# Latent attention with a paged cache: paged values and scores are moved directly behind the prompt's values, on TensorE

## The reference

```python
def latent_attention(q_abs, q_pe, c_kv, k_pe, q_pos, k_pos, w_uv):
    s = (jnp.einsum('bqhc,bkc->bhqk', q_abs, c_kv) + jnp.einsum('bqhr,bkr->bhqk', q_pe, k_pe)) * ATTN_SCALE
    s = jnp.where((k_pos[None, :] <= q_pos[:, None])[None, None], s, NEG_INF)
    p = jax.nn.softmax(s, axis=-1)
    o_lat = jnp.einsum('bhqk,bkc->bqhc', p, c_kv)
    return jnp.einsum('bqhc,chv->bqhv', o_lat, w_uv)
```

## Time and profile before

| | us |
|---|---|
| three runs, median (lowest, highest) | 2506.13 (2505.72, 2509.56) |
| span of the profiled execution, first to last instruction | 2500.6 |
| median less that span (the profiled execution has no time of its own beside its span) | 5.5 |
| attention loop, layer 1 (218.4 to 462.3) | 243.9, TensorE busy 235.9 |
| attention loop, layer 2 (1460.0 to 1704.3) | 244.3, TensorE busy 235.9 |

### The profile page before, as it was taken

One profiled execution on the slowest core, in us unless ns is written; L12 is line 12 of the kernel. 1 busy time (PEld: TensorE's weight loads), 2 busy tenths in 40 slices (PEclk: granted clock), 3 DMA queues, 4 the chain that ended last, 5 costly groups with the idle time before them and its releaser, 6 DMA issues.

```text
span 2500.6 us, 47127 instructions
## 1 busy us (share of the span) xinstructions
PE 2445.4 (98%) x18500; PEld 2197.3 (88%) x18500; DVE 1527.6 (61%) x1986; ACT 1025.4 (41%) x1535; POOL 926.5 (37%) x395
## 2 busy tenths in 40 slices
PE   8999999999999999999999999999999999999998
PEld 6996666897999999999979966668989999999998
DVE  5546666348776557655674566663497675567646
ACT  3224555327533333433441246552274333333334
POOL 2331000122664666455213310002136654665451
PEclk9999999999999999999999999999999999999999
DMA  6114322314545544663431143222236356445644
GB/s 224 55 39 119 94 86 81 119 59 149 199 161 213 204 157 152 214 217 142 148 113 50 35 130 89 87 87 109 75 126 252 145 182 232 165 151 180 223 141 154
DMA packets 182347, 347.40 MB, mean 139 GB/s; under 512 B 33969, under 2 KB 46449, under 8 KB 181425
## 3 DMA queue, kind: packets, MB, share of 16 engines
q1 hardware_dynamic: 116128, 207.12, 24.9%
q10 hardware_dynamic: 63504, 129.77, 14.3%
q0 software_dynamic: 2560, 8.39, 1.2%
HBM read 292.94 MB, written 49.06 MB: 137 GB/s over the span
## 4 chain that ended last, share of the span: by engine, by line
PE 81%; DVE 7%; ACT 4%; POOLq 3%; issue 2%; DVEq 1%; DMA 1%; POOL 1%; SPq 0%; ACTq 0%
PE psum L2926 21%; PE psum L2973 20%; PE psum L2428 12%; PE psum L2618 4%; PE psum L2413 3%; PE psum L2644 3%; PE psum L2458 3%; PE psum L2630 2%; PE psum L2521 2%; PE psum L2665 2%; PE psum L2477 2%; PE psum L2381 1%; ACT z L1174 1%; PE psum L2488 1%; PE psum L2678 1%
## 5 line engine op out<-in xcount | busy, mean ns | idle before, releaser
L2973 PE MATMUL psum<-hidh,wh 128*128 128x264 f32 x1312 | 374.2, 285 | 8.4 <-issue 5.9
L2973 PE MATMUL psum<-hidl,wh 128*128 128x264 f32 x1312 | 373.6, 285 | 0.0
L2973 PE MATMUL psum<-hidh,wl 128*128 128x264 f32 x1312 | 372.7, 284 | 0.0
L2926 PE MATMUL psum<-hh,wh 128*128 128x264 f32 x1280 | 363.4, 284 | 0.1
L2926 PE MATMUL psum<-hh,wl 128*128 128x264 f32 x1280 | 362.8, 283 | 0.0
L2926 PE MATMUL psum<-hl,wh 128*128 128x264 f32 x1280 | 362.6, 283 | 0.0
L2134 DVE TENSOR_TENSOR z<-psum,z 128x528 f32<-128x528 f32 x336 | 226.9, 700 | 94.1 <-PE psum L2973 94.1
L2973 PEld LDWEIGHTS psum<-hidh,wh 128*128 128x128 f32 x1312 | 246.5, 188 | 10.4 <-issue 7.0
L2973 PEld LDWEIGHTS psum<-hidh,wl 128*128 128x128 f32 x1312 | 247.2, 188 | 0.0
L2973 PEld LDWEIGHTS psum<-hidl,wh 128*128 128x128 f32 x1312 | 246.9, 188 | 0.0
L2926 PEld LDWEIGHTS psum<-hh,wh 128*128 128x128 f32 x1280 | 240.5, 188 | 0.5 <-issue 0.5
(11 more groups left out here) (329 smaller groups left out, 5935.0 us busy)
## 6 DMA issues: line engine op xcount, KB each, us to landing
hh<-h_quarters ACTq DMA_DIRECT2D x60, 1056.0 KB, 5.4
hl<-h_quarters ACTq DMA_DIRECT2D x60, 1056.0 KB, 7.5
raw<-wst SPq DMA_DIRECT2D x48, 512.0 KB, 3.6
z<-cache_c SPq DMA_DIRECT2D x352, 64.0 KB, 1.8
x<-x_spill SPq DMA_DIRECT2D x4, 4224.0 KB, 14.5
sacc<-wst SPq DMA_DIRECT2D x56, 256.0 KB, 3.2
t<-wst SPq DMA_DIRECT2D x56, 256.0 KB, 3.0
cn<-wst SPq DMA_DIRECT2D x56, 256.0 KB, 3.9
```

The lines of the kernel that those rows point to most:

```text
L2926: ins = pe.matmul(psum[:, up_bank(st, u) + q, 0:HW], w[:, o:o + P], m[part], start=(fresh and k == 0 and n == 0), stop=(k == 3 and n == 2) ...
L2973: ins = pe.matmul(psum[:, 2 * u + q, 0:HW], w[:, o:o + P], m[:, t, k * HB + q * HW:k * HB + q * HW + HW], start=(fresh and k == 0 and n == ...
```

## The change

On TensorE `step_values(c - 1)` moves from the end of phase 0 to directly behind `values`, and `step_scores(c)` from the end of phase 2 to directly behind `values` (at c = 0 and 8 behind `new_values`, which also moves forward). So tiles of 64 columns are followed by tiles of 32. `short` is dropped: `step_turn(c)` always stands in phase 3, and there `scores(i + 2, 1)` moves behind it. Bank 6 is divided by columns: prompt values in 0 to 127, paged values in 128 to 255. The paged matmuls no longer wait for bank 6 to be read; `values` still waits for both readers, and ScalarE's `take_o` now also waits for the paged values behind the prompt's, so that it does not read the bank while TensorE writes it. On VectorE phase 2 does `normalise`, `step_max`, then `take_pt` and `maxima`, instead of `take_pt`, `normalise`, `maxima`, `step_max`. On ScalarE `step_exp` moves from phase 3 to the end of phase 2.

```diff
@@ -279,6 +279,7 @@
 
         psum = ctx.enter_context(nc.psum_tensor("psum", [P, 8, 512], F32))
         ps = [psum[:, i, :] for i in range(8)]
+        prompt_o, paged_o = ps[6][:, 0:P], ps[6][:, P:2 * P]
 
         S = {}
 
@@ -1178,7 +1179,12 @@
 
                     u, j = JOBS[k]
                     act.wait_ge(o_full.sem, at.value(o_full, k + 1))
-                    act.activation(hh[:, u, tok(j)], ps[6][:, 0:P], ACT.Copy).then_inc(o_hi.sem, 1)
+                    c = (k + 1) // 2
+                    if k % 2 and k < len(JOBS) - 1:
+                        act.wait_ge(do_full.sem, at.value(do_full, out_of_step(c - 1)))
+                    if k % 2 == 0 and c % CHUNKS == 0:
+                        act.wait_ge(do_full.sem, at.value(do_full, out_of_step(c) - 1))
+                    act.activation(hh[:, u, tok(j)], prompt_o, ACT.Copy).then_inc(o_hi.sem, 1)
 
                 def take_pt(i):
 
@@ -1260,8 +1266,9 @@
                             if c == 0:
                                 act.wait_ge(outs.sem, at.value(outs, 64))
                             new_pt(c // CHUNKS)
+                    if ph == 2:
+                        step_exp(c)
                     if ph == 3:
-                        step_exp(c)
                         if i in K_AT and K_AT[i][1] == 0:
                             more_keys(K_AT[i][0])
                         step_pt(c)
@@ -1911,7 +1918,7 @@
 
                     u, j = JOBS[k]
                     dve.wait_ge(o_hi.sem, at.value(o_hi, k + 1))
-                    dve.tensor_tensor(hl[:, u, tok(j)], ps[6][:, 0:P], hh[:, u, tok(j)].bitcast(F32),
+                    dve.tensor_tensor(hl[:, u, tok(j)], prompt_o, hh[:, u, tok(j)].bitcast(F32),
                                       ALU.subtract).then_inc(o_new.sem, 1)
 
                 def take_pt(i):
@@ -1954,7 +1961,7 @@
                     dve.wait_ge(dexp.sem, at.value(dexp, first))
                     dve.tensor_copy(stat[:, 23:24], stat[:, 14:15])
                     dve.wait_ge(do_full.sem, at.value(do_full, first))
-                    dve.tensor_copy(oacc[quad], ps[6][:, 0:P]).then_inc(do_free.sem, 1)
+                    dve.tensor_copy(oacc[quad], paged_o).then_inc(do_free.sem, 1)
                     dve.drain()
 
                 def step_max(c):
@@ -1981,7 +1988,7 @@
                     quad = c // CHUNKS
                     dve.wait_ge(do_full.sem, at.value(do_full, out_of_step(c)))
                     dve.scalar_tensor_tensor(out=oacc[quad], in0=oacc[quad], scalar=stat[:, 6 + s:7 + s],
-                                             in1=ps[6][:, 0:P], op0=ALU.mult, op1=ALU.add).then_inc(do_free.sem, 1)
+                                             in1=paged_o, op0=ALU.mult, op1=ALU.add).then_inc(do_free.sem, 1)
                     dve.drain()
                     if c % CHUNKS == CHUNKS - 1:
                         dve.reciprocal(stat[:, 22:23], stat[:, 23:24])
@@ -2009,9 +2016,12 @@
                     big = JOBS[k][1] >= 4
                     if i % 2 == 0 and k > 0:
                         take_o(k - 1)
+                    if ph == 2:
+                        normalise(i + 1)
+                        step_max(c)
                     if big:
                         take_pt(i)
-                    if i + 1 < HALVES:
+                    if ph != 2 and i + 1 < HALVES:
                         normalise(i + 1)
                     if ph == 0 and c > 0:
                         take_ropes(c)
@@ -2027,10 +2037,8 @@
                             step_out(c - 1)
                         if c % CHUNKS == 0:
                             new_max(c // CHUNKS)
-                    if ph == 2:
-                        step_max(c)
-                        if c % CHUNKS == 0:
-                            new_out(c // CHUNKS)
+                    if ph == 2 and c % CHUNKS == 0:
+                        new_out(c // CHUNKS)
                     if ph == 3:
                         if i in K_AT and K_AT[i][1] == 1:
                             more_keys(K_AT[i][0])
@@ -2641,7 +2649,7 @@
                     pe.wait_ge(do_free.sem, at.value(do_free))
                     for kb in range(j + 1):
                         for e in range(2):
-                            ins = pe.matmul(ps[6][64 * e:64 * e + 64, 0:P],
+                            ins = pe.matmul(prompt_o[64 * e:64 * e + 64, :],
                                             vals[:, kb, (2 * u + e) * VD:(2 * u + e) * VD + VD],
                                             pts[2 * e + kb // 4][:, kb % 4, :], start=(kb == 0), stop=(kb == j),
                                             skip_group_check=True, tile_position=(0, 64 * e))
@@ -2678,10 +2686,6 @@
                     pe.matmul(ps[7][:, :], qrd[:, quad, :], rtt, start=False, stop=True,
                               skip_group_check=True).then_inc(ds_full.sem, 1)
 
-                def short(c):
-
-                    return c < STEPS - 1 and JOBS[2 * c + 1][1] + JOBS[2 * c + 2][1] < 7
-
                 def step_turn(c):
 
                     pe.wait_ge(dexp.sem, at.value(dexp, c + c // CHUNKS + 2))
@@ -2694,11 +2698,9 @@
 
                     s = c % CBUFS
                     evicted(RING_AT["x", c])
-                    pe.wait_ge(o_new.sem, at.value(o_new))
-                    pe.wait_ge(do_free.sem, at.value(do_free))
                     for r in range(4):
                         for b in range(QB):
-                            ins = pe.matmul(ps[6][rows_of(b), 0:P], ptd[:, r, rows_of(b)], cks[s][:, b, r, :],
+                            ins = pe.matmul(paged_o[rows_of(b), :], ptd[:, r, rows_of(b)], cks[s][:, b, r, :],
                                             start=(r == 0), stop=(r == 3), skip_group_check=True,
                                             tile_position=(0, 32 * b))
                     ins.then_inc(do_full.sem, 1)
@@ -2724,8 +2726,7 @@
 
                 def new_values(quad):
                     evicted(RING_AT["n", quad])
-                    pe.wait_ge(o_new.sem, at.value(o_new))
-                    pe.matmul(ps[6][:, 0:P], ptd[0:NS, 0, :], cn[0:NS, NB, 0:CL], start=True,
+                    pe.matmul(paged_o, ptd[0:NS, 0, :], cn[0:NS, NB, 0:CL], start=True,
                               stop=True).then_inc(do_full.sem, 1)
                     at.step(do_free)
 
@@ -2774,8 +2775,12 @@
                     next_big = i + 2 < HALVES and JOBS[k + 1][1] >= 4
                     if i % 2 == 0 and k > 0:
                         values(k - 1)
-                    if ph == 0 and c > 0 and short(c - 1):
-                        step_turn(c - 1)
+                    if ph == 0 and c > 0:
+                        step_values(c - 1)
+                    if ph == 2:
+                        if c % CHUNKS == 0:
+                            new_values(c // CHUNKS)
+                        step_scores(c)
                     turn_p(i, 0)
                     if i + 2 < HALVES:
                         scores(i + 2, 0)
@@ -2785,22 +2790,16 @@
                         turn_keys(c, 0)
                     if ph == 1:
                         turn_keys(c, 2)
-                    if next_big:
+                    if next_big and ph < 3:
                         scores(i + 2, 1)
                     if ph == 0:
                         turn_keys(c, 1)
-                        if c > 0:
-                            step_values(c - 1)
                         if c % CHUNKS == 0:
                             new_scores(c // CHUNKS)
                     if ph == 1:
                         turn_keys(c, 3)
                         if c % CHUNKS == 0:
                             new_turn(c // CHUNKS)
-                    if ph == 2:
-                        step_scores(c)
-                        if c % CHUNKS == 0:
-                            new_values(c // CHUNKS)
                     if ph == 3:
                         if i in K_AT:
                             u, h = K_AT[i]
@@ -2812,8 +2811,9 @@
                             pe.wait_ge(exped.sem, at.value(exped, HALVES))
                             pe.wait_ge(gate_l.sem, at.value(gate_l, NB + 1))
                             out_part(0, (4, 5, 6, 7))
-                        if not short(c):
-                            step_turn(c)
+                        step_turn(c)
+                        if next_big:
+                            scores(i + 2, 1)
                         if c == CHUNKS:
                             pe.wait_ge(on_new.sem, at.value(on_new, 1))
                             pe.transpose(ring(("f", 0))[:, 0:P], oacc[0], ident).then_inc(t_full.sem, 1)
@@ -2825,6 +2825,8 @@
                 evicted(len(RING) - 2)
                 evicted(len(RING) - 1)
                 out_part(1, (4, 5))
+                pe.wait_ge(o_new.sem, at.value(o_new))
+                pe.wait_ge(do_free.sem, at.value(do_free))
                 step_values(STEPS - 1)
                 out_part(1, (6, 7))
```

## The result

The changed kernel takes 2538.43 us (median of four runs, 2534.68 to 2538.83) against 2507.13 us for the kernel before on the same chip: a ratio of 1.0116, 95% interval 1.0102 to 1.013. I had forecast 2508.3 us and a range up to 2518. The change makes the kernel slower, by 31 us between the medians and by 29 us by the ratio.

The account below looks back on a forecast made before the run. TensorE, 98% busy, bounds the kernel, but VectorE and ScalarE chains limit the attention loop. Steps 0 to 11 -1.45, last pair +2.55: +1.1 us a layer, +2.2 on 2506.1 gives 2508.3 us; range 2503 to 2513, 8 in 10 2497 to 2518.

Parts of the forecast that it names:

- The cost of a change from 64 to 32 columns: TensorE between prompt values and paged tiles: taken as 0.15 us, with an upper bound of 0.25.
- The waits that would go: Five waits of the paged turn for its exponential, two of values for VectorE's copy: 4.5 us a layer saved.
- The new wait of the paged scores for the turned keys at j = 0 and 1: Phase 2, steps 4, 8 (j = 0) and 1, 5, 9 (j = 1): new waits of 0.56 and 0.25 us.
- the chain behind VectorE's copy: Phase 0, last pair: 3.9 us chain starts 1.01 us later; steps 12 to 14 longer, +2.55 us a layer.
- part (d) of the waits that come: Steps 0 to 11: VectorE's copy and next maximum, behind the paged maximum, come some 0.9 us later, delaying TensorE.
- the saving per pair in phase 0: Paged values directly behind prompt values: 0.16 us saved at each of 15 places a layer.
- the last pair's big halves: Steps 12 to 15, phase 2: paged scores moved forward bring one merge saving of 0.16 us, with no loss.
- step 15 come out even: Last step of the loop: limited by the exponential of the following half, so no growth.
- The next scores behind the paged turn: Phase 3: these scores start 0.6 us later, but all that follows moves by 1.0, so no cost.
- Rival 2: Chain decides everywhere: 1.01 us of paged values ahead of scores paid at all 15 places; +12 us, 2518; chance 0.28.
- that nothing changes outside the loops: Dense stages outside the attention loops, which no edit touches, keep their time; otherwise the prediction fails as a whole.
- the 5.5 us of the forecast: Whole kernel before: median of runs 5.5 us above the profiled 2500.6 us, taken as unchanged.

Follow-up runs that it names:

- experiment 1: Changed kernel with the paged values put back at the end of phase 0, nothing else undone: 2527.5 us, ratio 1.0075.
- Experiment 4: Changed kernel with ScalarE's copy of the turned block ahead of the next exponential in phase 3 alone: 2523.6 us, ratio 1.0048.
- Experiment 8: Kernel before with ScalarE's copy of the turned block ahead of the next exponential in phase 3: 2520.3 us, ratio 1.0051.
- experiment 7: Kernel before with bank 6 divided, paged turn always in phase 3, paged exponential one phase earlier, no paged matmul group moved: 2560.3 us, ratio 1.0214.
- experiment 12: Changed kernel with paged values back, ScalarE's copy first in phase 3, next scores ahead of the paged turn: 2512.3 us, ratio 1.0013.
- experiment 6: Kernel before with the paged values alone moved behind the prompt's, bank 6 divided, paged turn always in phase 3: 2525.1 us, ratio 1.0070.
- Experiment 13: Kernel before with only the paged values moved, in steps 1 to 11 alone: 2515.3 us, ratio 1.0031.
- Experiment 14: Kernel before with only the paged values moved, in steps 12 to 15 alone, paged turn always in phase 3: 2514.1 us, ratio 1.0021.

## Why the prediction was wrong

**Right.** The cost of a change from 64 to 32 columns (0.15 us). The waits that would go. The new wait of the paged scores for the turned keys at j = 0 and 1: 0.74 us at step 4, 0.35 and 0.34 at steps 1 and 5, forecast 0.56 and 0.25. In the last pair the chain behind VectorE's copy, its 1.0 us shift and the wait of L2665 (now L2673) for ScalarE's copy: steps 12 to 14 grew by 0.97, 1.15 and 1.17 us against 0.85, 0.8 and 0.9 forecast. At step 14 this is in part luck, as experiment 1 has 0.87 us of it with the values at their old place. The last pair's group grew by 3.66 us instead of 2.55.

**Wrong: part (d) of the waits that come, in head pairs 0 to 2.** I let the chain `maxima`, `exps`, `take_pt` end at the next `values` and priced it at 0.3 us for j = 2 and 0.7 to 0.8 elsewhere. The same `take_pt` also frees the ring place of the paged turn and the key product, which TensorE reaches 0.5 to 1.5 us before the values. Both then run after it in full instead of under it. So each of these steps paid one more turn or key product. Whole steps, with the paged turn of steps 3 and 7 booked to its own step as in the forecast, grew by 1.0 us (step 1), 1.4 to 1.5 (steps 4, 5, 8, 9), 0.5 to 0.6 (j = 2) and 0.6 to 0.8 (j = 3), where I had +0.3 to -0.5. The first three groups grew by 11.2 us a layer where -1.45 was forecast. Experiment 4 shows the mechanism: one exchange on ScalarE, which brings the copy forward, cuts the two waits by 8.2 us a layer and gives back 8.7 of the 11.3 us in second halves. Experiment 8 shows that the same exchange gains nothing where the wait doesn't exist.

**Wrong: the saving per pair in phase 0.** The merge did save 0.15 us (turns 0.27 to 0.22 and keys 0.53 to 0.43), yet the first halves of steps 1 to 11 changed by only -0.1 to +0.1 (but for steps 4 and 8). ScalarE's copy in phase 1 came 1 us later behind the big exponential, and the last turned keys waited for it through the same ring. I had shifted the chain by 1.0 us, and looked only at the copies of keys behind it.

**Underrated: the last pair's big halves.** I let step 15 come out even, and it grew by 0.37 us; and I let the paged scores in front of phase 2 cost nothing there but their merge. Experiment 1, where the values are back, shows +0.87 and +0.94 us in the first halves of steps 14 and 15. The next scores behind the paged turn, which I called neutral, show no price: experiments 7 and 12 have them at the old place and lose no less.

**Rivals.** Rival 2 had the sign and the kind of cause, independent work moved in front of a chain, but I priced it by the paged values at phase 0 alone (12 us), and there the first halves of steps 1 to 11 did not grow; the loss came at the second halves. With the paged values alone moved the kernel loses 17 us (experiment 6), with the scores alone 18 (experiment 1), with both 31, so the losses overlap. That they do since both delay the same copies is my reading and not tested.

**Wrong: that nothing changes outside the loops.** I wrote that the prediction fails as a whole if the dense stages change, and they did. The loops are 14.3 and 13.6 us longer, which leaves 3.4 us of the difference of the medians and 8.5 us of that of the two profiled spans. (The changed kernel's profiled run took 1.8 us more than its span. By the same 1.8 the profile of before is of an execution of some 2502.4 us, about 4 under its median, so the 5.5 us of the forecast were no constant.) Of the 8.5 us, 2.7 lie between the loops and 6.7 behind the last one, and these 6.7 arise between 187 and 232 us behind its last values, in the feed-forward part, where the same matmuls follow each other in both kernels. Four gaps of TensorE grew there by 3.5 us together, the first from 1.44 to 2.58 us. Right behind the first and the last of them the granted clock fell to the lower level, which it doesn't in the kernel before. From the page's 40 slices I had read that the clock was not at stake. The windows of this stretch, kernel before and then changed kernel (the third number from the end is the granted clock):

```profile
1894.00:1898.00 4.00, 2.56 (x22) 2.37 (x20) 3.80 (x1) 0.74 (x2) 1.59 (x1) 1.00 0.81 281
1898.00:1902.00 4.00, 4.00 (x33) 4.00 (x34) 1.42 (x2) 1.38 (x3) 0.00 (x0) 1.00 0.10 37
```

```profile
1925.00:1929.00 4.00, 1.43 (x12) 1.24 (x11) 2.46 (x1) 0.95 (x2) 0.25 (x1) 1.00 0.58 195
1929.00:1933.00 4.00, 4.00 (x22) 4.00 (x22) 0.71 (x1) 1.17 (x3) 0.00 (x0) 0.57 0.00 0
```

In 4 us of full work TensorE does 33 matmul records at the upper level and 22 in the window at 0.57, where they start 0.22 us apart for most of it instead of 0.12. The two stretches account for the remaining 3 us or so.

**Not settled.** Why these gaps grow. The part behind the start of the last values lasts 790.2 to 791.5 us in the six profiles with all paged values at the old place, and in none of them does the clock fall there before the last 5 us of the program. It lasts 794.8 to 798.0 in the eight with them moved. Experiments 13 and 14 gave 792.7 and 794.0, so it is no clean two-way split. In all these ten the clock falls at 227 to 231 us behind the start of the last values, and in six of them at 188 to 190 us too. The 2.7 us between the loops are within what the profiles of the other kernels differ by there (1000.0 to 1005.5 us).

## What to carry to other kernels

In this kernel, moving a group of matmuls next to another tiled group saved a fixed 0.15 us. Before doing it, ask what ran under the group at its old place: here 1 and 2 us of paged work covered a chain of VectorE and ScalarE, and 58 savings of 0.15 us came with a loss of 31 us. With a ring of two banks, price each late copy by its first waiter: whoever needs the place two turns on, not whoever reads the copied data. An order written out by hand on three engines is one schedule: single parts of this change, taken alone, cost 52 us (early exponential) or 96 us (VectorE's order undone). Waits can cost twice: read the granted clock by stage and not only on the page, whose 40 slices show 9 for both kernels.

## What the runs showed that I had not expected

The direct change between two column tilings costs the same as the way out to the whole array: 1.90 us for 32 records in both. A tiled group that waits restarts late: in step 5 ScalarE's copy (L1199) ends at 307.27 and the first of the paged scores starts at 307.56, 0.29 us later, while an ordinary turn starts 0.06 us behind its releaser (VectorE's normalise ends at 292.04 in the kernel before, the turn starts at 292.10). Whether the tiles or the number of semaphores awaited make the difference is not separated. An exchange of two instructions on ScalarE was worth -15 us in one order of TensorE and +12 us in the other.
